# Two-layer trunk with mixture-of-experts: expert rows weighed on GpSimd and added into the token rows in DRAM, with the first picks and the hand-off reordered

## What is computed

```python
def hier_moe(h, router_group, router_expert, w_gate, w_up, w_down):
    g_prob = softmax(xt @ router_group)                 # 4 groups, the best one is taken
    e_val, e_idx = lax.top_k(e_sel, 2)                  # the best two of its 8 experts
    gate = g_gate * softmax(e_val)                      # one weight for each of the two
    ...
    hb = silu(xb @ w_gate[e]) * (xb @ w_up[e])          # 1024 -> 512
    return hb @ w_down[e]                               # 512 -> 1024
    ...
    y = segment_sum(y_blocks * slot_w[:, None], slot_tok)   # weighed and added, token by token
```

## Time and profile before

| | us |
|---|---|
| Median of three runs (lowest, highest) | 1579.23 (1577.06, 1580.1) |
| The profiled execution, its own time | 1579.13 |
| Its span, first to last instruction | 1577.2 |
| Experts of layer 0, first gate product to last down product | 259.9 to 713.4 |
| Experts of layer 1, first gate product to last down product | 1102.5 to 1555.2 |
| Mean granted TensorE clock | 0.992 |

### The profile page before, as it was taken

One profiled execution on the slowest core, in us unless ns is written; L12 is line 12 of the kernel. 1 busy time (PEld: TensorE's weight loads), 2 busy tenths in 40 slices (PEclk: granted clock), 3 DMA queues, 4 the chain that ended last, 5 costly groups with the idle time before them and its releaser, 6 DMA issues. The chain is left out here.

```text
span 1577.2 us, 27525 instructions
## 1 busy us (share of the span) xinstructions
PE 1528.5 (97%) x11800; PEld 827.5 (52%) x11800; DVE 591.3 (37%) x1311; ACT 353.2 (22%) x583; POOL 273.2 (17%) x296
## 2 busy tenths in 40 slices
PE   8999999999999999998999999999999999999997
PEld 4887545544444444434666666646544444444442
DVE  5737634332322322225244444435322222222225
ACT  3152611100000000013445554431010000000003
POOL 9542000000000000000344444420000000000000
PEclk9999999999999999999999999999999999999999
DMA  6733086999999999995511121115999999999996
GB/s 222 270 85 120 14 360 244 406 424 428 427 426 427 427 427 425 429 417 221 214 54 55 62 89 66 54 72 209 384 417 427 426 427 427 427 425 427 427 422 264
DMA packets 63613, 472.24 MB, mean 299 GB/s; under 512 B 13041, under 2 KB 21241, under 8 KB 35584
## 3 DMA queue, kind: packets, MB, share of 16 engines
q1 hardware_dynamic: 58544, 462.52, 71.3%
q0 software_dynamic: 4800, 7.87, 1.3%
q10 hardware_dynamic: 144, 0.05, 0.0%
HBM read 452.03 MB, written 24.27 MB: 302 GB/s over the span
## 5 line engine op out<-in xcount | busy, mean ns | idle before, releaser
L929 PE MATMUL ps<-sb_ring,sb_work 128*56 128x512 f32 x2048 | 454.6, 596 | 16.3 <-issue 14.1
L929 PEld LDWEIGHTS ps<-sb_ring,sb_work 128*56 128x56 f32 x2048 | 147.0, 131 | 310.4 <-issue 310.1
L944 PE MATMUL ps<-sb_ring,sb_work 128*56 128x512 f32 x1024 | 230.8, 593 | 0.0
L1632 POOL DMA_INDIRECT expert_rows<-sb_work,sb_ri x60 | 54.7, 912 | 997.9 <-DVE sb_work L2112 712.7
L712 PEld LDWEIGHTS ps<-sb_work,sb_h 128*64 128x64 f32 x4096 | 206.1, 138 | 34.4 <-issue 30.8
L712 PE MATMUL ps<-sb_work,sb_h 128*64 128x112 f32 x4096 | 223.8, 263 | 0.0
L2103 DVE TENSOR_TENSOR sb_work<-sb_work,ps 56x512 f32<-56x512 f32 x64 | 70.3, 1099 | 317.9 <-ACT sb_work L1429 317.8
L1170 PE MATMUL ps<-sb_work,sb_ring 128*128 128x512 f32 x384 | 173.7, 607 | 2.0 <-ACT sb_work L1304 2.0
L1429 ACT ACTIVATE sb_work<-ps 56x512 f32<-56x512 f32 x64 | 37.6, 588 | 436.6 <-PE ps L929 436.5
L944 PEld LDWEIGHTS ps<-sb_ring,sb_work 128*56 128x56 f32 x1024 | 67.1, 130 | 112.9 <-issue 112.5
L1444 ACT ACTIVATE sb_work<-ps 56x512 f32<-56x512 f32 x60 | 35.4, 590 | 393.7 <-PE ps L944 355.7
(11 more groups left out here) (255 smaller groups left out, 1348.6 us busy)
## 6 DMA issues: line engine op xcount, KB each, us to landing
sb_ring<-in_w_down_dram SPq DMA_DIRECT2D x62, 2048.0 KB, 24.6
sb_ring<-in_w_gate_dram SPq DMA_DIRECT2D x54, 2048.0 KB, 22.2
sb_ring<-in_w_up_dram SPq DMA_DIRECT2D x54, 2048.0 KB, 25.8
sb_ring<-in_w_gate_dram SPq DMA_DIRECT2D x18, 1024.0 KB, 10.6
sb_ring<-in_w_up_dram SPq DMA_DIRECT2D x18, 1024.0 KB, 29.0
sb_ring<-in_c_w_in_dram SPq DMA_DIRECT2D x8, 2048.0 KB, 8.2
sb_ring<-in_ab_w_in_dram SPq DMA_DIRECT2D x8, 1024.0 KB, 9.5
expert_rows<-sb_work SPq DMA_DIRECT2D x2, 4096.0 KB, 21.3
```

What stands on the lines that cost most here:

```text
L929: mm = nc.tensor.matmul(dst[64 * z:64 * z + CAP, :], me["xgT"][:, j, c, q * CAP:(q + 1) * CAP], wblock(slots[z], NC)[:, c, :], start=(c == ...
L944: mm = nc.tensor.matmul(dst[64 * z:64 * z + CAP, :], src[:, c * CAP:(c + 1) * CAP], wblock(slots[2], FC)[:, c, z * 512:(z + 1) * 512], sta ...
L1632: return g.indirect_dma_start(out=y_d[l], out_offset=bass.IndirectOffsetOnAxis(ap=idx, axis=0), in_=me["rows"][0:CAP, j, :], in_offset=Non ...
```

## The change

- The DRAM tensor has one row for each token (T rows, `token_rows`). SP stores `h` there, 512 KB for each tile, once the mixer's output is added (`store_tokens`), after the weight loads of expert 2. The zero fill of the old tensor is gone, with its memset.
- `tokval` gives both choices of a token the same row. A second table of slots, `slot_gate`, holds the gate of each slot: 8 more small products in `slot_table`, two more DVE products in `slot_lists`, one more copy in `row_table`.
- For each expert 0 to 29, GpSimd first multiplies the 56 x 1,024 rows by their gates in place, waits for that, waits for the scatter of the expert before it, and then issues a scatter that adds to the row in DRAM.
- `rows_back` waits for all scatters and for the last picks and loads the 4 tiles (512 KB each) into `h` itself. `combine`, `add_rows` and the diagonal matrices are gone. `add_late` waits for the tile's load.
- The exponentials of the gates are made in `mixer_end` and the gates before expert 0, where they came in expert 3.
- In `out_proj` the first half of `pick_first(l, 2)` stands before `positions` of tile 3.
- Of the last expert ACT copies one half and DVE the other, where ACT copied both.
- Hand-off: PE turns tiles 0 and 1, then runs the value projection of head 0 tile by tile with the turning of tiles 2 and 3 between, and then the other three projections. ACT copies the turned tile 0 before it squares tile 3. The loads of the projection weights 0 and 1 follow `rows_back` at once.

```diff
-        y_d = [nc.dram_tensor(f"expert_rows{l}", [2 * T, D], F32).ap() for l in range(2)]
+        y_d = [nc.dram_tensor(f"token_rows{l}", [T, D], F32).ap() for l in range(2)]
...
-            for l in range(2):
-                sp.dma_start(y_d[l].rearrange("(a p) d -> p a d", p=P),
-                             zeros.unsqueeze(1).broadcast_to([P, 2 * NT, D])).then_inc(zero_out, 16)
...
+            def store_tokens(l):
+
+                for t in range(NT):
+                    for nb in range(2):
+                        wait_drained(sp, ("out", l, t, nb))
+                    sp.dma_start(y_d[l][t * P:(t + 1) * P, :], h[:, t, :]).then_inc(h_stored, 16)
...
             def rows_back(l):
 
                 sp.wait_ge(ov_done, l + 1)
-                back = y_d[l].rearrange("(k t p) d -> t p k d", k=2, t=NT)
+                for b in range(PB):
+                    wait_full(sp, ("pick", l, NK // PICK, b))
                 for t in range(NT):
-                    wait_full(sp, ("gu" if t < 2 else "dn", l, NS + 1))
-                    sp.dma_start(yrow(t), back[t]).then_inc(yrow_in[t], 16)
+                    sp.dma_start(h[:, t, :], y_d[l][t * P:(t + 1) * P, :]).then_inc(h_back[t], 16)
...
-                if i == 1:
-                    sp.wait_ge(h_ready, 4)
+                if i < 2:
+                    wait_full(sp, ("gu", 0, NS + 1))
...
                 pick_first(l, 1)
+                pick_first(l, 2, range(0, 4))
                 positions(l, NT - 1)
-                pick_first(l, 2)
+                pick_first(l, 2, range(4, 8))
...
-                for t in range(NT - 1):
+                for t in range(NT):
                     late_add(l, t)
-                add_rows(l, NT - 2, (0,))
-                late_add(l, NT - 1)
-                add_rows(l, NT - 1, (0, 1))
...
-            turn_rows(2)
-            xT_ready(2)
-            for H in range(HEADS_C + 2):
+            turn_rows(2, (0, 1))
+            s, n = w1_in[0]
+            pe.wait_ge(ring_in[s], 16 * n)
+            opens(("c", 0, 2))
+            for t in range(NT):
+                xT_ready(2, (t,))
+                mm = proj_v(0, t)
+                if t + 2 < NT:
+                    turn_rows(2, (t + 2,))
+            fills(mm, ("c", 0, 2))
+            for k in (0, 1, 3):
+                proj1(0, k)
+            for H in range(1, HEADS_C + 2):
...
                     square(2, t, h[:, t, :], junk2)
-                take_turned(2, 0)
+                    if t == NT - 2:
+                        wait_full(act, ("add", 0, NT - 1, 1))
+                        take_turned(2, 0)
                 take_turned(2, 1)
...
-                drains(keep_rows(l, d, 1), ("dn", l, d))
...
                 return g.indirect_dma_start(out=y_d[l], out_offset=bass.IndirectOffsetOnAxis(ap=idx, axis=0),
                                             in_=me["rows"][0:CAP, j, :], in_offset=None,
-                                            bounds_check=2 * T - 1, oob_is_err=False)
+                                            bounds_check=T - 1, oob_is_err=False, compute_op=ALU.add)
...
-                pool.wait_ge(zero_out, 32)
+                pool.wait_ge(h_stored, 16 * NT * (l + 1))
                 for e in range(NK):
                     wait_drained(pool, ("dn", l, e))
+                    own = me["rows"][0:CAP, e % 2, :]
+                    g.tensor_scalar(own, own, me["slot_gate"][0:CAP, e:e + 1], None, ALU.mult).then_inc(weighed, 1)
+                    pool.wait_ge(weighed, l * NK + e + 1)
+                    if e > 0:
+                        pool.wait_ge(scattered[(e - 1) % 2], 16 * (l * (NK // 2) + (e - 1) // 2 + 1))
                     scatter_rows(l, e % 2, ri[:, e:e + 1]).then_inc(scattered[e % 2], 16)
...
             def add_late(l, t):
 
+                dve.wait_ge(h_back[t], 16 * (l + 1))
                 for nb in range(2):
...
                 selections(l, 1)
+                gate_values(l)
                 for e in range(NS):
                     dve_expert(l, e)
                 last_experts(l)
-                combine(l, 0)
-                combine(l, 1)
                 if l == 0:
                     add_late(l, 0)
                     add_late(l, 1)
                     norm_col(2, 0)
                     norm_rows(2, 0)
-                    combine(l, 2, (1,))
+                    add_late(l, 2)
                     norm_col(2, 1)
                     norm_rows(2, 1)
-                    add_late(l, 2)
                     add_late(l, 3)
...
                 else:
-                    combine(l, 2, (1,))
                     add_late(l, 0)
```

More of the change, by code:

```diff
@@ L954, in slot_table @@
                 for i in range(2 * NT):
-                    mm = nc.tensor.matmul(dst[0:CAP, 0:NE], me["A"][:, i // NT, i % NT, :],
-                                          me["B"][:, i // NT, i % NT, :], start=(i == 0), stop=(i == 2 * NT - 1))
+                    nc.tensor.matmul(dst[0:CAP, 0:NE], me["A"][:, i // NT, i % NT, :],
+                                     me["B"][:, i // NT, i % NT, :], start=(i == 0), stop=(i == 2 * NT - 1))
+                for i in range(2 * NT):
+                    mm = nc.tensor.matmul(dst[0:CAP, NE:2 * NE], me["A"][:, i // NT, i % NT, :],
+                                          me["G"][:, i // NT, i % NT, :], start=(i == 0), stop=(i == 2 * NT - 1))
                 fills(mm, ("tab", l))
@@ L1093, in late_add @@
                     dst = opens(job)
[L1094 to L1102, removed]
-                for nb in range(2):
-                    for k in ks:
-                        mm = nc.tensor.matmul(bank(("add", l, t, nb))[:], diag[:, k if t == NT - 1 else 2, :],
-                                              yrow(t)[:, k, nb * 512:(nb + 1) * 512], start=False, stop=(k == ks[-1]))
-                    fills(mm, ("add", l, t, nb))
+                    fills(nc.tensor.matmul(dst[:], late_pick[:, t * P:(t + 1) * P],
+                                           me["rows"][:, 1, nb * 512:(nb + 1) * 512], start=True, stop=True), job)
             def more_blocks(l):
@@ L1146, in moe, with proj_v @@
                 last_experts(l)
-                for t in range(NT - 1):
+                for t in range(NT):
                     late_add(l, t)
-                add_rows(l, NT - 2, (0,))
-                late_add(l, NT - 1)
-                add_rows(l, NT - 1, (0, 1))
             moe(0)
+            def proj_v(H, t):
+                w = ring[:, w1_in[H][0], :].rearrange("p (c k n) -> p c k n", c=NC, k=4)
+                for c in range(NC):
+                    mm = halves(bank(("c", H, 2))[:, t * P:(t + 1) * P], xT[:, c, t * P:(t + 1) * P], w[:, c, 2, :],
+                                c == 0, c == NC - 1)
+                return mm
             def proj1(H, k):
@@ L1164, in proj1 @@
                     for t in range(NT):
-                        for c in range(NC):
-                            mm = halves(dst[:, t * P:(t + 1) * P], xT[:, c, t * P:(t + 1) * P], w[:, c, k, :],
-                                        c == 0, c == NC - 1)
+                        mm = proj_v(H, t)
                 else:
@@ L2177, in last_experts @@
                 late_selections(l).then_inc(late_ready, 1)
-                for k in range(2):
-                    v.tensor_scalar(diag[:, k, :], ident[:], gates[:, k, NT - 1:NT], None, ALU.mult)
-                v.tensor_scalar(diag[:, 2, :], ident[:], gates[:, 0, NT - 2:NT - 1], None, ALU.mult
-                                ).then_inc(late_ready, 1)
                 last_hidden(l, c)
@@ L2256, in more_blocks @@
                     dve.wait_ge(o["scatter"], NE * per_e * 16)
-            def combine(l, t, ks=(0, 1)):
-                dve.wait_ge(yrow_in[t], 16 * (l + 1))
-                for k in ks:
-                    v.scalar_tensor_tensor(out=h[:, t, :], in0=yrow(t)[:, k, :], scalar=gates[:, k, t:t + 1],
-                                           in1=h[:, t, :], op0=ALU.mult, op1=ALU.add).then_inc(h_ready, 1)
-                    dve.wait_ge(h_ready, l * (2 * NT - 3) + 2 * t + k - ks[0] + 1)
             def final_rows(t, first):
```

67 lines of the change are left out of this document (38 added, 29 removed).

## The result

| | before | after |
|---|---|---|
| Median of 20 runs each (lowest, highest), us | 1578.4 (1573.24, 1581.17) | 1582.16 (1577.55, 1586.26) |
| Ratio after / before, 95% interval | | 1.003, 1.0022 to 1.0038 |
| Span of the profiled execution, us | 1577.2 | 1580.8 |
| F of layer 0 (end of its last down product) | 713.4 | 721.8 |
| First gate product of layer 1 | 1102.5 | 1100.3 |

The change costs 0.3%, 3.8 us by the medians and 3.6 by the profiled spans, where 8 were forecast. The spans split into five stretches: up to the first gate product of layer 0 +0.4, experts of layer 0 +8.0, from there to the first gate product of layer 1 -10.6, experts of layer 1 +9.5, the end -3.75. Together +3.6.

What follows compares the result with a forecast made beforehand. The prediction took the DMAs to bound the expert stretches, PE and hand-offs the rest. Layer 0: +8.6 - 0.9 - 6.0 = +1.7; layer 1: +8.6 + 0.6 - 2.9 = +6.3; together +8.0 on 1579.1, 1587 us, own range 1582 to 1592, whole 1566 to 1602.

Steps and rivals of the forecast that it cites:

- What bounds the experts: Expert stretches: DMAs fall behind PE by 1.1 us an expert, so DMA time added there is paid one for one.
- The price of adding: Scatters in the experts: reading the old rows costs 0.31 us each, 28 count, +8.6 us in each layer.
- The free read: Rival, expert scatters: old rows are read while the weight stream waits elsewhere, sum -9.2, 1570 us; chance 0.32.
- the slow add: Rival, expert scatters: read, add and write in line, three times the price, +42; twice likelier, 1604 us; chance 0.10.
- half the price: Rival, expert scatters: reads partly overlap, 0.16 us a scatter, sum -0.6, 1578 to 1579 us; chance 0.10.
- The estimate from that page: Expert scatters: by the skill page's ratio of 1.93, adding would cost 8.0 us extra a layer.
- First picks: PE's wait for the choice of tile 3: half a `pick_first` fills 0.9 us, -0.9 in layer 0, 0 in layer 1.
- The hand-off in layer 0: End of layer 0's experts to the projections: -6.0 us, bounds 0 and -8.9, the slow start's 2.9 taken at nothing.
- The end of layer 1: After layer 1's last down product: the last ACT copy ends at F + 16.0 instead of F + 18.9, -2.9 us.
- GpSimd: Experts: weighing of some 3.1 us and scatters in line stay hidden, all landed by about F - 8; cost 0.
- the rival of late scatters: Layer ends: landings of 12 us or more cost 1.5 to 5 us a layer; 0.08 together with no hand-off gain.
- The store: Token rows stored before the experts, 4.9 us of DMA time: 0 in layer 0, +0.6 us in layer 1.

Runs made afterwards that it cites:

- e1: The kernel after with its adding scatter made plain again, GpSimd's weighing kept; median 1567.86 us, ratio to before 0.9919.
- e5: The kernel after without GpSimd's weighing, rows scattered with addition but without their gates; median 1581.13 us, ratio to before 1.0019.
- e6: The kernel after with the old order of the hand-off, all tiles turned first; median 1584.98 us, ratio to before 1.0036.
- e4: The kernel before with the new order of the first picks alone; median 1574.5 us, ratio to before 0.9975.
- e2: The kernel before with its scatter made adding, nothing else changed; median 1593.41 us, ratio to before 1.0087.
- e7: The kernel before with every expert's rows scattered a second time, plainly, into a spare tensor; median 1596.87 us, ratio to before 1.0112.
- e8: The kernel before with the new order of the hand-off alone, `combine` kept; median 1575.5 us, ratio to before 0.9977.
- e3: The kernel before with both new orders, first picks and hand-off, without the adding; median 1569.65 us, ratio to before 0.9942.
- e10: The kernel before with both new orders, the same kernel run again on another chip; median 1572.34 us, ratio to before 0.9968.
- e9: The kernel before with both new orders and the store of the token rows into spare tensors; median 1572.05 us, ratio to before 0.9963.

## Why the prediction was right, and where its terms were off

**What bounds the experts** was right. DMA share is at 1.01, the waits begin earlier, and the last down product of layer 0 ends 8.45 us later where 7.7 were foretold; adding in the kernel before and a second plain pass both went into the expert stretches (+16.6 us where the span grew by 15.6, +20.4 where it grew by 20.1), and the other stretches moved by 3 us or less.

**The price of adding** was right: 0.31 us a scatter, 17.2 in all, against 14.3 by medians and 14.9 by spans in the kernel after, 14.5 and 15.6 in the kernel before. The engine time is 0.34 us by the shares, 20.5 us for 60 scatters, so 70 to 76% of it reached the end; what absorbs the rest was not tried. The free read and the slow add fall, and half the price (8.6 us) too. The Trainium skill, page "Collectives: The Full Stack", section "The bandwidth ceiling: the fold count and why AG ≠ RS ≠ AR", gives the ratio 1.93 for a collective that adds against one that copies. The estimate from that page was 16.0 us in all. The share's doubling (1.3 to 2.6%) and the measured 14.3 to 15.6 us agree with it. The reason that the page gives, a second read through one queue, no run here shows.

**First picks** are one of two steps that were mis-sized: -0.9 in layer 0 and 0 in layer 1. The step counted the wait and named the clock only as a bound. SP's issue of expert 2's up weights, first for layer 0 and layer 1 in the kernel before, then in the kernel after, lets the picks be read apart from what comes ahead of them:

```profile
246.27 0.33 SPq L508 DMA_DIRECT2D sb_ring<-in_w_up_dram  x1
...
1089.12 0.33 SPq L508 DMA_DIRECT2D sb_ring<-in_w_up_dram  x1
```

```profile
248.91 0.33 SPq L497 DMA_DIRECT2D sb_ring<-in_w_up_dram  x1
...
1088.12 0.33 SPq L497 DMA_DIRECT2D sb_ring<-in_w_up_dram  x1
```

To the first gate product it took 13.61 and 13.35 us before, 11.41 and 12.18 after: -2.2 in layer 0 and -1.2 in layer 1. In layer 0 the clock no longer fell; in layer 1 it still did. The first gate product of layer 0 came 0.4 us later all the same, because the kernel after was already 2.6 us behind at 248.91, most of it by the fall of the clock at 192 us; in e1, e5 and e6, the same code up to there, the experts start 1.2 to 1.7 us earlier than before. By the run alone the picks are worth -4.3 us. That run has no store in the DMAs' gap, so it does not test the 0 for layer 1, whose reason was that the store leaves no gap.

**The hand-off in layer 0** was set at -6.0, one sum for the order and the dropped `combine`, with the clock's 2.9 at nothing. The engines' part came out as summed: the value projection ends at 743.31, F + 21.5 where F + 21.8 was summed, so 20.5 - (21.5 - 7.35) = -6.35. From F of layer 0 to SP's issue of the up weights in layer 1 it took 375.7 us before and 366.3 after: -9.45. The missing 3.1 are close to the 2.9 that the prediction had priced for the slow start of the projections and taken at nothing, so the step that failed is this term; the upper bound of -8.9 was the better value. In 732 to 739 the clock went from 0.59 to 1.00. The same distance in the other profiles is 374.3 with `combine` and the old order (e4, e2, e7: 374.25 to 374.4), 371.3 with the new order (e8, e3, e10, e9), 368.2 without `combine` (e6) and 366.3 with both (after, e1, e5). So in this change the dropped `combine` gives 5 to 6 us and the order 2 to 3; they overlap by 1.

**The end of layer 1** was set at -2.9 and gave -3.75. The lines of the kernel after that answer to the earlier trace rows:

```profile
1558.08 4.50 PE L943 MATMUL ps<-sb_ring,sb_work 128*56 128x512 f32 x20
...
1576.52 1.22 ACT L1332 ACTIVATE sb_ring<-sb_ring,sb_rstd 128x512 f32<-128x512 f32 x1 [1.44 <-DVE sb_rstd L1746]
```

The last copy ends at 1577.74, F + 15.2, where F + 16.0 was summed. From F to the end of the span it is 18.2 us in every kernel without `combine` and 21.6 to 22.1 in every one with it.

**GpSimd** was costed at nothing. The product takes 2.98 us (3.1 forecast), a landing 9.1 us (8 to 9). The last scatters of layer 0, GpSimd and SP's queue, answering to the earlier trace rows:

```profile
692.12 2.85 POOL L1648 TENSOR_SCALAR sb_work<-sb_work 56x1024 f32<-56x1024 f32 x1 [18.96 <-DVE sb_work L2133]
695.89 1.47 POOL L1638 DMA_INDIRECT token_rows<-sb_work,sb_ri  x1 [0.92 <-POOL sb_work L1648]
696.92 3.35 POOL L1648 TENSOR_SCALAR sb_work<-sb_work 56x1024 f32<-56x1024 f32 x1
705.65 1.47 POOL L1638 DMA_INDIRECT token_rows<-sb_work,sb_ri  x1 [5.38 <-DMA token_rows<-sb_work,sb_ri]
...
714.35 1.98 SPq L606 DMA_DIRECT2D sb_h<-token_rows  x4
```

Everything had landed by 714.35, F - 7.5, where F - 8 was summed; the rival of late scatters decides only from F - 2.7. The run without weighing agrees.

**The store** was 0 and +0.6, and the run with the store and both orders cannot tell it from 0.

**The sum.** +8.0 was forecast, +3.8 measured; 1582.16 us lies at the very edge of the forecast's own range, 1582 to 1592, so that it fell inside is close to luck. By medians, adding came out 2.9 us cheaper (14.3 for 17.2), and all the rest of the change is worth -11.0 (the kernel after with a plain scatter against before; -8.7 to -16.7 by the interval of the ratio) instead of -9.2. By the stretches of the two profiled executions the expert stretches cost 17.5 where 17.8 were forecast for scatter and store, and most of the miss lies between the layers, -10.6 for -6.0. The two views differ because in e1, without the adding, the expert stretches still cost 5.6 us more than before. So that the two expert stretches came out to 0.3 us is partly luck: the price per scatter was somewhat high, and something that the prediction had at 0 filled the difference. **What stays open** is that something. Both orders (5.9 to 9.2), the end (3.75) and the dropped `combine` between the layers (4 to 5 by the stretches) would make 14 to 18 by themselves, against -11.0 by the medians; the interval of the ratio reaches into that range, so part of the gap can be noise. Neither the store nor the weighing shows a loss of that size. The scatters in line and the table of gates were not tried alone.

## What to carry to other kernels

Where the DMA share is at its ceiling, price an indirect DMA with addition as two passes of its rows, and ask what the extra pass displaces; here that was 15 us, more than all that the dropped weighing, loading and zero fill gave back. Take the parts of a change apart before judging it: the two orders of instructions, which have nothing to do with the adding, are worth 0.3 to 0.6% by themselves and made its price look like a fraction of what it is. A short wait of PE should be read together with the granted clock behind it: 0.8 us less of waiting in each layer gained 4.3 us, of which the wait itself explains some 0.5 a layer.

## What the runs showed that was not expected

- **The clock answers to sub-microsecond changes of a wait, but not every time.** In the twelve profiles, the granted clock fell to its lower level (1.2 GHz) behind the wait for the last choice in layer 0 in four of four kernels with the 2.0 us wait and in one of eight with 1.25 us (e9, window 252 to 262 at 0.83). In layer 1 it fell in two of four (before, e2) and in two of eight (after, e5). At the start of the projections it fell in the four kernels with both `combine` and the old order, and in none of the other eight. Behind a wait of 1.5 us at 192 us, the same in all twelve, it fell in three (after, e7, e9). So a shorter wait makes the fall rarer and does not exclude it. The mean clock also goes with the spread between executions of one kernel: in the 14 runs of the kernel before that stand beside e1, e2, e3 and e6, the time went from 1575.4 us at 0.997 to 1584.5 at 0.990.
- **DVE beside GpSimd.** The select of 128 x 56 takes 307 ns in the kernel before, 559 in the kernel after and 316 in the same kernel without GpSimd's products. It cost nothing that can be measured here, where DVE is busy 40% of the span. Whether a kernel bound by DVE pays it was not tried.
- **GpSimd's issue of an adding scatter** takes 1.47 us where the plain one takes 0.91; the landing goes from 7.9 to 9.1 us (8.8 in the kernel before with adding alone).
